# Shift and scale of the conditioning by output columns: two chunks of channels at a time, against all eight at once

## The chip, the cores and the metric

The kernel runs on one core of one Trainium2 chip. The metric is the device time of one execution in microseconds; the median of three runs is given. Views of the trace come from one profiled execution.

## The reference, cut to what matters

One layer of a streaming encoder, for a prompt of 2048 tokens with one conditioning vector and for 8 sample sequences of 16 tokens with one vector each. All is float32, with a width of 1024.

```python
def _layer(x, c, ...):
    mod = jax.nn.silu(c) @ w_ada + b_ada                 # w_ada: 1024 x 6144
    sh1, sc1, gt1, sh2, sc2, gt2 = [m[:, None, :] for m in jnp.split(mod, 6, axis=-1)]
    h = _rmsnorm(x, g_pre_mix) * (1 + sc1) + sh1
    proj = h @ w_in                                      # 17 units of 128 output channels
    ...                                                  # pooling, 31-tap convolution, short convolution
    mix = jnp.concatenate([ya, yb, yc], axis=-1) @ w_out
    x = x + gt1 * _rmsnorm(mix, g_post_mix)
    h = _rmsnorm(x, g_pre_ffn) * (1 + sc2) + sh2
    f = (jax.nn.silu(h @ w_gate) * (h @ w_up)) @ w_down
    return x + gt2 * _rmsnorm(f, g_post_ffn), ...
```

## The kernel before, in words

The 17 tiles of 128 tokens (1 of samples, 16 of the prompt) are worked in six blocks, the first of two tiles and the others of three. Every weight is streamed again for each block, as units of 128 x 1024, through a ring of six places (`raw`, `wlo` in the same memory, and `whi`). SP issues all loads, in an order written out by hand. A unit's place is loaded again once `w_used` counts its last reader. ScalarE makes the high part of a unit (`high(n)`, line 788), VectorE the rest (`low(n)`, line 1141), and TensorE (PE) takes three matmuls for each product of 128 rows: high by high, high by low, low by high (line 518). `ahead(...)` makes both parts four units ahead.

Each engine runs its own queue in program order and waits on semaphores. The modulation comes from `w_ada`: `ada_units` (line 539) multiplies four chunks of 128 input channels at a time, in four strips of the array, and leaves partial sums in four strips of PSUM; `ada_out` on ScalarE (line 939) copies them to `mod`; `ada_columns` (line 518) adds the four strips by a matmul with a matrix of ones and turns the result to channels by rows; `columns` on VectorE (lines 1152 to 1156) adds the bias and makes the scale. Parts 0 and 1 (shift and scale of the first norm) need the first sixteen units of `w_ada`, of 512 KB each. They go to `raw`, `h_pre` and `pr`. The others come later in fours, between projections.

For each chunk k of 128 channels of a block, `transposes(q, k)` on PE (line 573) turns the normalised x to channels by tokens in PSUM bank k % 2. In block 0 VectorE then scales and shifts the samples' tokens (`modulate_samples`, lines 1175 and 1177), ScalarE the prompt's (`modulate`, line 843) and splits off the high part (`h_split`, line 850), and VectorE makes the rest (`h_rest`, line 1183). `project(b, j)` is one unit of `w_in`. Its result is copied out of PSUM by `evacuate(b, j)` on ScalarE (lines 859 to 866), and unit j + 2 waits for that.

The convolutions and the pooling of a block are one generator on VectorE, `mixing(b)`, with 148 steps in block 0 (a step is one operation of the generator, the taps at line 1274 most of them). `advance(mixer, n)` takes n steps of it between other work. Its constants: `IN_FIRST` steps for each of the 15 units with an `ahead` in block 0, and again behind each of the four units in `FOUR_IN`; `IN_BETWEEN` steps before each `h_rest(1, k)`; `IN_EARLY` steps after each of four `low` while block 1's first units are projected; then `finish(mixer)` takes what is left. Pooling is the last part of it. On PE `statistics(0, i)` stand behind `project(1, 3)` and wait for `pooled_ready` and `z_ready`, which the generator signals; behind them come `project(1, 4)`, `gate_rows(0)`, `statistics(0, 3)`, `project(1, 5)`, `gate_rows(1)` and the first output projection, `mix_out(0, 0)`.

Of the kernel before, what the change touches and what calls it, by code (L numbers as in the profile page):

```python
# [11 lines left out]
P = 128  # L12
# [54 lines left out]

PRE = 2 * KD
PART_READ = {part: n for n, part in enumerate((0, 1, 3, 4, 2, 5))}
# [34 lines left out]
IN_FIRST, IN_BETWEEN, IN_EARLY, IN_OUT = 5, 3, 6, 2  # L104
# [13 lines left out]
E_END = E_FOLD + ROWS + 1  # L118
# [60 lines left out]
def build(nc, x_all, c_all, consts, consts_a, cols, gpost, b_ada, w_ada, w_mix, w_pool, w_gu, w_dn,  # L179
# [3 lines left out]
    with ctx:  # L183
# [8 lines left out]
        with ExitStack() as under:  # L192
            h_pre = sb("h_pre", [P, 2 * TB, D], scope=under, align=OPERAND)
# [59 lines left out]
        pre_landed = [sem(f"pre_landed{i}") for i in range(PRE)]  # L253
# [63 lines left out]
        def pre(i):  # L317

            if i < RING:
                return raw[:, i, :]  # L320
            i -= RING
            if i < 2 * TB:
                return h_pre[:, i, :]
            i -= 2 * TB
            return pr[:, :, :].rearrange("p s n -> p (s n)")[:, i * D:(i + 1) * D]

# [28 lines left out]

        def gu_bank(m, i):
            return (6 if m % 2 else 0) + i
# [4 lines left out]
        def _(sp):  # L362
# [34 lines left out]
            for i in range(STRIPS):  # L397
                sp.dma_start(pre(i), w_ada[i]).then_inc(pre_landed[i], 16)
# [5 lines left out]
            for i in range(STRIPS, PRE):  # L404
                sp.dma_start(pre(i), w_ada[i]).then_inc(pre_landed[i], 16)  # L405
# [37 lines left out]
            sp.wait_ge(cols_full, 2)  # L443
# [72 lines left out]
        def _(pe):  # L516
# [6 lines left out]
            def ada_units(q):  # L523

                g, k0 = STRIPS * q // KD, STRIPS * q % KD
                if k0 == 0 and g > 1:
                    pe.wait_ge(ada_read, PART_READ[g] - 1)
                if q >= PRE // STRIPS:
                    pe.wait_ge(four_landed[FOURS.index(q)], 16 * STRIPS)
                for h in range(2):  # L530
                    for i in range(STRIPS):
                        at, strip = STRIPS * q + i, C_PAD * i
                        if at < PRE:
                            src = pre(at)
                            if h == 0:
                                pe.wait_ge(pre_landed[at], 16)
                        else:
                            src = four_place(FOURS.index(q), i)
                        last = nc.tensor.matmul(ps[strip:strip + C_PAD, 2 + 2 * ADA_PAIR[g] + h, :], c_s[:, k0 + i, :],  # L539
                                                src[:, 512 * h:512 * h + 512], start=k0 == 0,  # L540
                                                stop=k0 + STRIPS == KD, tile_position=(0, strip), skip_group_check=True)
                        if h and at < PRE:
                            last.then_inc(pre_used, 1)
                if q >= PRE // STRIPS:
                    last.then_inc(four_used, 1)

            def ada_columns(bank):
                for i in range(2):
                    for k in range(KD):
                        o = (i * KD + k) * (ROWS + 1)  # L550
                        last = mm(ps[:, bank, o:o + ROWS + 1], mod[:, i, k * P:(k + 1) * P],
                                  con_a[0:MOD_K, E_FOLD:E_FOLD + ROWS + 1], True, True)
                last.then_inc(cols_full, 1)

            def gate_rows(i):

                e, row = E_SELP if i % 2 else E_SELS, PART_ROW[5 if i >= 2 else 2]
                pe.wait_ge(ada_read, PART_READ[5 if i >= 2 else 2] + 1)
                if i:
                    pe.wait_ge(gates_made, i)  # L560
                else:
                    pe.wait_ge(mod_ready, 4)
# [25 lines left out]
            def project(b, j):  # L588
                n, q, w = UNIT["in", b, j], norm("M", b), NT[b] * P
                if j >= 2:  # L590
                    pe.wait_ge(evac_done, evac_count(b, j - 2))
                elif b == 1:
# [4 lines left out]
                by_columns(n, ps[:, j % 2, 0:w], q, w, j == 0)  # L597
# [70 lines left out]
            def statistics(b, i):  # L668
# [3 lines left out]
                if i < NPOOL:  # L672
                    if b == 0 and i == 0:
                        pe.wait_ge(w_pool_landed, 16 * len(WINDOWS))
                        pe.wait_ge(ada_read, 6)
# [19 lines left out]
            for q in range(3):  # L695
                ada_units(q)
            pe.wait_ge(const_landed, 48)
            transposes(0, 0)
            transposes(0, 1)
            ada_units(3)  # L700
            pe.wait_ge(bias_landed[0], 16)
            pe.wait_ge(ada_read, 2)
            ada_columns(6)
            for k in range(2, KD):
                transposes(0, k)
            for j in range(NIN):
                project(0, j)
                if j in FOUR_IN:
                    ada_units(FOURS[FOUR_IN[j]])
# [3 lines left out]
            ada_units(FOURS[4])  # L713
# [3 lines left out]
            pe.wait_ge(ada_read, 4)  # L717
            ada_columns(7)
            for k in range(5, KD - 1):
                transposes(1, k)  # L720
            ada_units(FOURS[5])
# [3 lines left out]
            ada_units(FOURS[FOUR_EARLY[1]])  # L725
            project(1, 2)
            project(1, 3)
            ada_units(FOURS[FOUR_EARLY[3]])
# [53 lines left out]
        def _(act):  # L782
# [50 lines left out]
            def modulate(q, k):  # L833
                kind, b = NORMS[q]
                ph, w, c0 = int(kind == "F"), NT[b] * P, P if b == 0 else 0
                if k == 0:
                    act.wait_ge(mod_ready, 2 + 2 * ph)
# [14 lines left out]
            def evacuate(b, j):  # L852
# [3 lines left out]
                src = ps[:, j % 2, 0:w]  # L856
# [74 lines left out]
            nc.scalar.activation(c_s[:, :, 0:ROWS], c_sb[:, :, :], ACT.Silu).then_inc(c_ready, 1)  # L931
            def ada_out(g):
                if g < 2:
                    act.wait_ge(pre_used, KD * g + KD)
                else:
                    act.wait_ge(four_used, FOURS.index(2 * g + 1) + 1)
                if g > 2:
                    act.wait_ge(cols_full, 2 if g == 5 else 1)
# [7 lines left out]
            ada_out(0)  # L946
            ada_out(1)
            for n in range(LEAD):
                high(n)
            for k in range(KD):  # L950
                modulate(0, k)
                h_split(0, k)
                if k >= KD - 2:
                    high(LEAD + k - (KD - 2))
# [170 lines left out]
        def _(dve):  # L1125
# [22 lines left out]
            def columns(i, bank):  # L1148
                dve.wait_ge(cols_full, i + 1)
                src = ps[:, bank, 0:2 * KD * (ROWS + 1)].rearrange("p (n m) -> p n m", m=ROWS + 1)  # L1150
                dst = shsc[:, 2 * i:2 * i + 2, :, :].rearrange("p i k r -> p (i k) r")
                after(own.step(nc.vector.tensor_copy(dst, src[:, :, 0:ROWS])))
                tt(dst, dst, src[:, :, ROWS:ROWS + 1].to_broadcast([P, 2 * KD, ROWS]), ALU.add).then_inc(mod_ready, 1)
                g0 = (Q_G1, Q_G2)[i]
                dve.wait_ge(mod_ready, (1, 3)[i])
                stt(shsc[:, 2 * i + 1, :, :], shsc[:, 2 * i + 1, :, :], 1.0,
                    col[:, g0:g0 + KD].unsqueeze(2).to_broadcast([P, KD, ROWS]), ALU.add, ALU.mult)\
                    .then_inc(mod_ready, 1)
# [7 lines left out]
            def modulate_samples(q, k):  # L1166
                ph = int(NORMS[q][0] == "F")
                if k == 0:
                    dve.wait_ge(mod_ready, 2 + 2 * ph)
# [288 lines left out]
            for k in range(KD):  # L1458
# [16 lines left out]
            for k in range(KD):  # L1475
                advance(mixer, IN_BETWEEN)
                h_rest(1, k)
                if k == 5:
                    columns(1, 7)
# [178 lines left out]
```

## Time and profile before

| | us |
|---|---|
| median of three runs | 2311.78 (2310.27 to 2313.1) |
| the profiled execution's own time | 2310.73 |
| its span in the trace | 2308.9 |
| PE busy (matmul) | 2261.1, 98% of the span |
| VectorE busy | 1350.8, 59% |
| ScalarE busy | 1027.1, 44% |
| mean granted clock of TensorE | 0.99 |

The span runs from the first to the last record of the trace. A busy share is an average over the span; a stretch in which PE is idle has to be looked for in the time slices and the waits. The granted clock is the share of 2.4 GHz that PE got.

### The profile page before, as it was taken

How to read it: one execution, taken by the hardware profiler on the slowest of the kernel's cores; microseconds unless marked ns; L12 is line 12 of the kernel's file. 1: busy time of each engine (PE TensorE's matmuls, PEld its weight loads, DVE VectorE, ACT ScalarE, POOL GpSimd, SP SyncE). 2: the span in 40 equal slices, each digit the busy share in tenths (PEclk: the TensorE clock that was granted, in tenths of full speed). 3: DMA queues.
4: the chain of work that ended last, by engine and by line, in shares of the span. 5: the costliest groups of instructions: out<-in, count | busy, mean ns of one | idle time of the engine just before them, and what ended most of it. 6: DMA issues, size and time to landing. Idle time of an engine off the chain costs nothing.

```text
span 2308.9 us, 30258 instructions
## 1 busy us (share of the span) xinstructions
PE 2261.1 (98%) x12444; PEld 2084.0 (90%) x12444; DVE 1350.8 (59%) x1937; ACT 1027.1 (44%) x1432; POOL 41.6 (2%) x82
## 2 busy tenths in 40 slices
PE   7899999999999999999999999999999999999998
PEld 3779898988999998999998899989889997899987
DVE  3969885589453577744367764346784534443343
ACT  4554455545353534444353436344443424433332
POOL 0000000000000000000000000000000000000000
PEclk8999999999999999999999999999999999999999
DMA  8845454444533353453343354335335433444332
GB/s 334 335 151 173 166 201 153 158 171 164 183 125 122 127 183 120 155 174 127 128 176 127 127 183 146 128 119 182 128 123 178 127 125 117 173 153 155 128 128 91
DMA packets 101743, 361.64 MB, mean 157 GB/s; under 512 B 12259, under 2 KB 14435, under 8 KB 101604
## 3 DMA queue, kind: packets, MB, share of 16 engines
q1 hardware_dynamic: 101606, 359.71, 44.4%
q8 instruction: 99, 1.62, 0.3%
q14 instruction: 38, 0.31, 0.0%
HBM read 340.73 MB, written 18.93 MB: 156 GB/s over the span
## 4 chain that ended last, share of the span: by engine, by line
PE 90%; DVE 6%; DMA 2%; ACT 1%; SPq 1%; issue 0%; POOL 0%; POOLq 0%; DVEq 0%; ACTq 0%
PE ps L518 89%; DVE pr L1274 2%; DVE wlo L1141 2%; PE ps L573 1%; DMA raw<-in_w_mix 1%; DMA pr<-in_w_ada 1%; PE ps L539 0%; DVE h_lo L1183 0%; DVE g_lo L1190 0%; DMA raw<-in_w_gu 0%; SPq L405 0%; ACT whi L788 0%; DVE xr L1214 0%; ACT h_f L843 0%; DVE h_f L1175 0%
## 5 line engine op out<-in xcount | busy, mean ns | idle before, releaser
L1141 DVE TENSOR_TENSOR wlo<-raw,whi 128x1024 fp32r<-128x1024 f32 x546 | 665.1, 1223 | 524.8 <-ACT whi L788 523.6
L518 PE MATMUL ps<-h_hi,whi 128*128 128x384 f32 (+1 forms) x2928 | 960.0, 328 | 1.6 <-ACT h_f L843 1.6
L518 PE MATMUL ps<-h_lo,whi 128*128 128x384 f32 (+1 forms) x2928 | 954.8, 326 | 0.0
L518 PE MATMUL ps<-h_hi,wlo 128*128 128x384 f32 (+1 forms) x2928 | 954.8, 326 | 0.0
L788 ACT ACTIVATE whi<-raw 128x1024 fp32r<-128x1024 f32 x546 | 575.5, 1057 | 779.1 <-DMA raw<-in_w_gu 528.1
L518 PEld LDWEIGHTS ps<-h_hi,whi 128*128 128x128 f32 x2928 | 553.3, 189 | 9.1 <-issue 4.7
L518 PEld LDWEIGHTS ps<-h_lo,whi 128*128 128x128 f32 x2928 | 553.3, 189 | 2.2 <-issue 0.5
L518 PEld LDWEIGHTS ps<-h_hi,wlo 128*128 128x128 f32 x2928 | 553.2, 189 | 0.0
L518 PE MATMUL ps<-whi,g_hi 128*128 128x512 f32 x748 | 235.9, 396 | 7.0 <-DVE g_lo L1190 5.5
L518 PE MATMUL ps<-whi,g_lo 128*128 128x512 f32 x748 | 231.6, 391 | 0.0
L518 PE MATMUL ps<-wlo,g_hi 128*128 128x512 f32 x748 | 231.2, 390 | 0.0
L1274 DVE SCALAR_TENSOR_TENSOR pr<-u,col,pr 128x384 f32<-128x384 f32 x360 | 208.8, 614 | 0.9
L1565 DVE TENSOR_TENSOR g_f<-ps,s_buf 128x384 f32<-128x384 f32 (+1 forms) x132 | 70.5, 534 | 222.4 <-PE ps L518 222.2
L518 PEld LDWEIGHTS ps<-whi,g_hi 128*128 128x128 f32 x748 | 137.3, 189 | 36.7 <-DVE g_lo L1190 9.8
L518 PEld LDWEIGHTS ps<-wlo,g_hi 128*128 128x128 f32 x748 | 140.7, 188 | 30.0
L518 PEld LDWEIGHTS ps<-whi,g_lo 128*128 128x128 f32 x748 | 140.7, 188 | 29.8
L843 ACT ACTIVATE h_f<-ps,shsc 128x384 f32<-128x384 f32 (+1 forms) x96 | 61.0, 635 | 223.3 <-PE ps L573 196.7
L1183 DVE TENSOR_TENSOR h_lo<-h_f,h_hi 128x384 fp32r<-128x384 f32 (+1 forms) x96 | 51.4, 535 | 154.2 <-ACT h_hi L850 154.2
L518 PE MATMUL ps<-whi,y_pr 128*128 128x512 f32 x476 | 137.2, 395 | 0.0
L859 ACT ACTIVATE pr<-ps 128x384 f32<-128x384 f32 (+1 forms) x84 | 39.4, 469 | 146.1 <-PE ps L518 146.1
L518 PEld LDWEIGHTS ps<-whi,y_pr 128*128 128x128 f32 x476 | 87.8, 188 | 17.6 <-issue 0.5
L1190 DVE TENSOR_TENSOR g_lo<-g_f,g_hi 128x384 fp32r<-128x384 f32 (+1 forms) x132 | 70.1, 531 | 11.3 <-ACT g_hi L927 11.3
(127 smaller groups left out, 1192.7 us busy)
## 6 DMA issues: line engine op xcount, KB each, us to landing
raw<-in_w_gu SPq DMA_DIRECT2D x264, 512.0 KB, 3.2
raw<-in_w_mix SPq DMA_DIRECT2D x150, 512.0 KB, 3.3
raw<-in_w_dn SPq DMA_DIRECT2D x132, 512.0 KB, 3.2
xt<-in_x_all SPq DMA_DIRECT2D x17, 512.0 KB, 5.9
xr<-in_x_all SPq DMA_DIRECT2D x17, 512.0 KB, 6.0
xr<-x_all SPq DMA_DIRECT2D x17, 512.0 KB, 5.6
x_all<-xr SPq DMA_DIRECT2D x5, 1536.0 KB, 7.5
xr<-in_w_ada SPq DMA_DIRECT2D x12, 512.0 KB, 6.8
```

The source lines that it names most:

```text
L518: return nc.tensor.matmul(out, lhsT, rhs, start=start, stop=stop, skip_group_check=True)
L573: last = nc.tensor.transpose(ps[:, k % 2, t * P:(t + 1) * P], xt[:, t, k * P:(k + 1) * P], ident)
L788: nc.scalar.activation(whi[:, s, :], raw[:, s, :], ACT.Copy).then_inc(w_hi, 1)
L843: nc.scalar.activation(h_f[:, k % 2, c0:w], ps[:, k % 2, c0:w], ACT.Identity, scale=shsc[:, 2 * ph + 1, k, 0:1], bias=shsc[:, 2 * ph, k, 0 ...
L859: i = nc.scalar.activation(dst, src, ACT.Sigmoid if kind == "g" else ACT.Copy)
L1141: tt(wlo[:, s, :], raw[:, s, :], whi[:, s, :].bitcast(F32), ALU.subtract).then_inc(w_lo, 1)
L1183: tt(h_lo[:, k, 0:w], h_f[:, k % 2, 0:w], h_hi[:, k, 0:w].bitcast(F32), ALU.subtract)\
L1190: tt(g_lo[:, s, 0:w], g_f[:, k, 0:w], g_hi[:, s, 0:w].bitcast(F32), ALU.subtract).then_inc(g_lo_ready, 1)
L1274: i = stt(z, conv_in(j, k), wk, src, ALU.mult, ALU.add)
L1565: tt(g_f[:, m, 0:w], ps[:, gu_bank(m, 1), 0:w], s_buf[:, m % 2, 0:w], ALU.mult).then_inc(g_ready, 1)
```

## The change

The first sixteen units of `w_ada` are laid out in DRAM by output columns: four groups of four units, a group holding all input channels for two chunks of shift and two of scale. `ada_group(g)` multiplies a group whole (8 matmuls of 512 columns) into one PSUM bank of its own; `group_out(g)` copies that bank; `group_columns(g)` takes 4 small matmuls for the two chunks; `columns` takes the same two chunks. Each group's chunks are transposed, modulated and split while the next group lands. The bias is added by the matmul itself, so that `columns` has two operations and not three. The landing place is one tensor, `pre`, over `h_hi`, `h_lo`, `raw` and a part of `pr`. Units 0 and 1 of block 0 go to PSUM banks 2 and 3. Further, `high` and `low` of units 0 to 5 stand at the last group and behind it, the states are loaded behind unit 5 instead of unit 3, `load_x(1)` stands behind unit 8 instead of unit 5, and `IN_FIRST` goes from 5 to 4 and `IN_BETWEEN` from 3 to 1.

```diff
-PART_READ = {part: n for n, part in enumerate((0, 1, 3, 4, 2, 5))}
+GROUPS = PRE // STRIPS
+PART_READ = {part: GROUPS + 1 + n for n, part in enumerate((3, 4, 2, 5))}
...
-IN_FIRST, IN_BETWEEN, IN_EARLY, IN_OUT = 5, 3, 6, 2
+IN_FIRST, IN_BETWEEN, IN_EARLY, IN_OUT = 4, 1, 6, 2
...
-            h_pre = sb("h_pre", [P, 2 * TB, D], scope=under, align=OPERAND)
+            pre = sb("pre", [P, PRE, D], scope=under, align=OPERAND)
...
+        def in_bank(b, j):
+
+            return j % 2 + (2 if b == 0 and j < 2 else 0)
...
-                    sp.wait_ge(pre_used, n + 1)
+                    sp.wait_ge(pre_used, (2 * TB + n) // STRIPS + 1)
...
-                if j == 3:
+                if j == RING - 1:
                     sp.dma_start(u_s[:, :, 0:SEQS, :], st_conv).then_inc(state_landed, 16)
...
                 if j == RING - 1:
                     load_four(0)
-                    sp.wait_ge(t_full, KD)
-                    load_x(1)
                 if j == 7:
                     load_four(1)
                 if j == 8:
-                    sp.wait_ge(cols_full, 1)
+                    sp.wait_ge(t_full, KD)
+                    load_x(1)
+                    sp.wait_ge(cols_full, GROUPS)
...
+            def ada_group(g):
+
+                pe.wait_ge(pre_landed[g], 16 * STRIPS)
+                for k in range(KD):
+                    strip = C_PAD * (k % STRIPS)
+                    out = ps[strip:strip + C_PAD, 2 + g, :].rearrange("p (a n) -> p a n", a=STRIPS)
+                    last = nc.tensor.matmul(out, c_s[:, k, :], pre[:, STRIPS * g:STRIPS * g + STRIPS, k * P:(k + 1) * P],
+                                            start=k < STRIPS, stop=k >= STRIPS, tile_position=(0, strip),
+                                            skip_group_check=True)
+                last.then_inc(pre_used, 1)
...
+            def group_columns(g):
+                pe.wait_ge(ada_read, g + 1)
+                if g >= 2:
+                    pe.wait_ge(mod_ready, 2 * (g - 1))
+                ada_columns(6 + g % 2, (2 * g, 2 * g + 1))
...
-            for q in range(3):
-                ada_units(q)
+            ada_group(0)
             pe.wait_ge(const_landed, 48)
-            transposes(0, 0)
-            transposes(0, 1)
-            ada_units(3)
             pe.wait_ge(bias_landed[0], 16)
-            pe.wait_ge(ada_read, 2)
-            ada_columns(6)
-            for k in range(2, KD):
-                transposes(0, k)
+            for g in range(GROUPS):
+                group_columns(g)
+                if g + 1 < GROUPS:
+                    ada_group(g + 1)
+                transposes(0, 2 * g)
+                transposes(0, 2 * g + 1)
...
+            def group_out(g):
+                act.wait_ge(pre_used, g + 1)
+                src = ps[0:BIAS, 2 + g, :].rearrange("p (i n) -> p i n", i=2)
+                nc.scalar.activation(mod[0:BIAS, 0:2, 2 * P * g:2 * P * (g + 1)], src, ACT.Copy).then_inc(ada_read, 1)
...
+            group_out(0)
             for t in range(NT[0]):
                 x_square(0, t)
             for t in range(NT[0]):
                 x_normalise(0, t)
-            ada_out(0)
-            ada_out(1)
-            for n in range(LEAD):
+            for g in range(GROUPS):
+                if g:
+                    group_out(g)
+                if g == GROUPS - 1:
+                    high(0)
+                for k in (2 * g, 2 * g + 1):
+                    modulate(0, k)
+                    h_split(0, k)
+            for n in range(1, RING):
                 high(n)
...
-            for n in range(2):
-                low(n)
-            columns(0, 6)
-            modulate_samples(0, 0)
-            for k in range(KD):
-                if k + 1 < KD:
-                    modulate_samples(0, k + 1)
-                h_rest(0, k)
-                if k in (3, 5):
-                    low(2 + k // 5)
-            for n in range(LEAD, RING):
+            for g in range(GROUPS):
+                columns(0, 6 + g % 2, (2 * g, 2 * g + 1))
+                modulate_samples(0, 2 * g)
+                modulate_samples(0, 2 * g + 1)
+                if g == GROUPS - 1:
+                    low(0)
+                h_rest(0, 2 * g)
+                h_rest(0, 2 * g + 1)
+            for n in range(1, RING):
                 low(n)
...
-    wa = np.asarray(w_ada)[0].reshape(KD, P, 6, D).transpose(2, 0, 1, 3).reshape(6 * KD, P, D)
+    wa = np.asarray(w_ada)[0].reshape(KD, P, 6, D).transpose(2, 0, 1, 3)
+    wa_groups = wa[:2].reshape(2, KD, P, GROUPS, 2, P).transpose(3, 0, 4, 2, 1, 5).reshape(PRE, P, D)
+    wa = np.concatenate([wa_groups, wa[2:].reshape(4 * KD, P, D)])
```

## Rows read from the trace of the kernel before

**Rows 1.** The page, busy time of each engine over the span.
```profile
PE 2261.1 (98%) x12444; PEld 2084.0 (90%) x12444; DVE 1350.8 (59%) x1937; ACT 1027.1 (44%) x1432; POOL 41.6 (2%) x82
```
**Rows 2.** Stretches: length, then PE, PEld, DVE, ACT, POOL busy, clock, DMA share, GB/s.
```profile
65.88:113.11 47.23, 42.82 (x353) 34.97 (x344) 47.16 (x101) 27.02 (x42) 2.14 (x2) 0.98 0.87 321
118.55:148.17 29.62, 28.86 (x170) 22.73 (x169) 20.16 (x56) 10.14 (x15) 0.00 (x0) 0.89 0.30 107
...
167.02:2308.90 2141.88, 2120.62 (x11574) 1979.52 (x11572) 1248.41 (x1702) 948.38 (x1309) 37.78 (x72) 1.00 0.42 147
```
**Rows 3.** Waits of PE, 50 to 400 us: total, times, longest.
```profile
PE ps L573 <- ACT h_f L843: 8.7, 7, 5.2
```
**Rows 4.** Chain of waits in order of time, 0 to 140 us: start, length, what.
```profile
12.93 14.97 DMA pr<-in_w_ada
...
29.89 1.03 ACT mod L939
...
31.05 5.05 PE ps L518 x32
...
45.87 10.82 PE ps L518 x72
...
56.71 8.06 DMA raw<-in_w_mix
```
**Rows 5.** Timeline of PE, 0 to 75 us: start, length, operation, idle before.
```profile
17.95 0.62 PE L539 MATMUL ps<-h_pre,c_s 128*32 128x512 f32 x1 [0.16 <-DMA h_pre<-in_w_ada]
...
24.77 0.66 PE L573 MATMUL ps<-con,xt 128*128 128x128 f32 x4
```
**Rows 6.** Timeline of ACT (ScalarE), 0 to 75 us.
```profile
15.61 2.19 ACT L817 ACTIVATE xt<-xt,rstd_x 128x1024 f32<-128x1024 f32 x2 [1.16 <-POOL rstd_x L1081]
...
37.81 0.46 ACT L843 ACTIVATE h_f<-ps,shsc 128x128 f32<-128x128 f32 x1 [3.12 <-DVE h_f L1177]
...
39.10 0.42 ACT L850 ACTIVATE h_hi<-h_f 128x256 fp32r<-128x256 f32 x1
```
**Rows 7.** Timeline of DVE (VectorE), 0 to 185 us.
```profile
37.08 0.29 DVE L1175 TENSOR_TENSOR h_f<-ps,shsc 128x128 f32<-128x128 f32 x1
...
65.88 1.23 DVE L1141 TENSOR_TENSOR wlo<-raw,whi 128x1024 fp32r<-128x1024 f32 x1 [3.93 <-ACT whi L788]
...
143.78 1.23 DVE L1141 TENSOR_TENSOR wlo<-raw,whi 128x1024 fp32r<-128x1024 f32 x1 [3.14 <-ACT whi L788]
...
147.11 0.60 DVE L1352 SCALAR_TENSOR_TENSOR pr<-wsum,xa 64x128 f32<-64x128 f32 x2
```
**Rows 8.** Stretches of 1 us, as rows 2; the clock is the third number from the end.
```profile
33.00:34.00 1.00, 1.00 (x7) 1.00 (x7) 1.00 (x2) 1.00 (x2) 0.00 (x0) 0.59 1.11 388
...
111.00:112.00 1.00, 0.00 (x0) 0.00 (x0) 1.00 (x5) 0.00 (x0) 0.00 (x0) 0.84 1.03 410
```
**Rows 9.** Timeline of PE, 100 to 205 us.
```profile
105.70 0.87 PE L573 MATMUL ps<-con,xt 128*128 128x128 f32 x6 [0.54 <-ACT xa L864]
...
149.48 1.10 PE L518 MATMUL ps<-pr,w_pl 128*128 128x256 f32 x4 [1.19 <-issue]
...
160.14 1.56 PE L518 MATMUL ps<-pr,con_a 128*128 128x256 f32 x6 [2.38 <-ACT pr L885]
...
167.02 1.03 PE L518 MATMUL ps<-whi,y_pr 128*128 128x512 f32 x2
```
**Rows 10.** Chain of waits in order of time, 100 to 170 us.
```profile
114.48 0.90 PE ps L573 x3
115.39 6.63 PE ps L518 x32
...
127.46 8.60 PE ps L518 x48
...
146.43 1.90 PE ps L539 x16
...
150.14 7.57 DMA raw<-in_w_mix
```

More of the change, by code:

```diff
@@ L252, in build @@
         w_pool_landed = sem("w_pool_landed")
-        pre_landed = [sem(f"pre_landed{i}") for i in range(PRE)]
+        pre_landed = [sem(f"pre_landed{i}") for i in range(GROUPS)]
         pre_used = sem("pre_used")
@@ L397, in _ @@
             for i in range(STRIPS):
-                sp.dma_start(pre(i), w_ada[i]).then_inc(pre_landed[i], 16)
+                sp.dma_start(pre[:, i, :], w_ada[i]).then_inc(pre_landed[0], 16)
             load_x(0)
@@ L404, in _ @@
             for i in range(STRIPS, PRE):
-                sp.dma_start(pre(i), w_ada[i]).then_inc(pre_landed[i], 16)
+                sp.dma_start(pre[:, i, :], w_ada[i]).then_inc(pre_landed[i // STRIPS], 16)
             def load_four(f):
@@ L525, in ada_units @@
+            def ada_units(f):
+                q = FOURS[f]
                 g, k0 = STRIPS * q // KD, STRIPS * q % KD
[L526 to L529, printed above, removed]
+                if k0 == 0:
+                    pe.wait_ge(ada_read, max(GROUPS, PART_READ[g] - 2))
+                pe.wait_ge(four_landed[f], 16 * STRIPS)
                 for h in range(2):
@@ L531, in ada_units @@
                     for i in range(STRIPS):
[L532 to L538, printed above, removed]
+                        strip = C_PAD * i
                         last = nc.tensor.matmul(ps[strip:strip + C_PAD, 2 + 2 * ADA_PAIR[g] + h, :], c_s[:, k0 + i, :],
-                                                src[:, 512 * h:512 * h + 512], start=k0 == 0,
+                                                four_place(f, i)[:, 512 * h:512 * h + 512], start=k0 == 0,
@@ L541, in ada_units, with ada_columns @@
                                                 stop=k0 + STRIPS == KD, tile_position=(0, strip), skip_group_check=True)
[L542 to L547, printed above, removed]
+                last.then_inc(four_used, 1)
+            def ada_columns(bank, ks):
                 for i in range(2):
-                    for k in range(KD):
-                        o = (i * KD + k) * (ROWS + 1)
-                        last = mm(ps[:, bank, o:o + ROWS + 1], mod[:, i, k * P:(k + 1) * P],
-                                  con_a[0:MOD_K, E_FOLD:E_FOLD + ROWS + 1], True, True)
+                    for n, k in enumerate(ks):
+                        o = (i * len(ks) + n) * ROWS
+                        last = mm(ps[:, bank, o:o + ROWS], mod[:, i, k * P:(k + 1) * P],
+                                  con_a[0:MOD_K, E_FOLD:E_FOLD + ROWS], True, True)
@@ L591, in project @@
                     pe.wait_ge(evac_done, evac_count(b, j - 2))
+                elif b == 0:
+                    pe.wait_ge(ada_read, j + 1)
                 elif b == 1:
@@ L712, in _ @@
             transposes(1, 1)
-            ada_units(FOURS[4])
+            ada_units(4)
             for k in range(2, 5):
@@ L716, in _ @@
             pe.wait_ge(bias_landed[1], 16)
-            pe.wait_ge(ada_read, 4)
-            ada_columns(7)
+            pe.wait_ge(ada_read, PART_READ[4])
+            ada_columns(7, range(KD))
             for k in range(5, KD - 1):
                 transposes(1, k)
-            ada_units(FOURS[5])
+            ada_units(5)
             transposes(1, KD - 1)
@@ L724, in _ @@
             project(1, 1)
-            ada_units(FOURS[FOUR_EARLY[1]])
+            ada_units(FOUR_EARLY[1])
             project(1, 2)
             project(1, 3)
-            ada_units(FOURS[FOUR_EARLY[3]])
+            ada_units(FOUR_EARLY[3])
             for i in range(3):
@@ L835, in modulate @@
                 ph, w, c0 = int(kind == "F"), NT[b] * P, P if b == 0 else 0
-                if k == 0:
-                    act.wait_ge(mod_ready, 2 + 2 * ph)
+                if q == 0:
+                    act.wait_ge(mod_ready, 2 * (k // 2) + 2)
+                elif k == 0:
+                    act.wait_ge(mod_ready, 2 * GROUPS + 2 * ph)
                 act.wait_ge(t_full, KD * q + k + 1)
@@ L945, in _ @@
                 x_normalise(0, t)
-            ada_out(0)
-            ada_out(1)
-            for n in range(LEAD):
-                high(n)
[L950 to L954, printed above, removed]
+            for g in range(GROUPS):
[7 more added lines that the diff above has]
+            for n in range(1, RING):
+                high(n)
             for j in range(NIN):
@@ L1146, in ahead, with columns @@
                     low(n)
[L1148 to L1158, printed above, removed]
+            def columns(i, bank, ks):
+                n = len(ks)
+                dve.wait_ge(cols_full, ks[0] // 2 + 1 if i == 0 else GROUPS + 1)
+                src = ps[:, bank, 0:2 * n * ROWS].rearrange("p (i k r) -> p i k r", i=2, r=ROWS)
+                at, g0 = slice(ks[0], ks[0] + n), (Q_G1, Q_G2)[i] + ks[0]
+                nc.vector.tensor_copy(shsc[:, 2 * i, at, :], src[:, 0, :, :]).then_inc(mod_ready, 1)
+                stt(shsc[:, 2 * i + 1, at, :], src[:, 1, :, :], 1.0,
+                    col[:, g0:g0 + n].unsqueeze(2).to_broadcast([P, n, ROWS]), ALU.add, ALU.mult).then_inc(mod_ready, 1)
             def gate(i, bank):
@@ L1167, in modulate_samples @@
                 ph = int(NORMS[q][0] == "F")
-                if k == 0:
-                    dve.wait_ge(mod_ready, 2 + 2 * ph)
+                if k % 2 == 0 if q == 0 else k == 0:
+                    dve.wait_ge(mod_ready, 2 * GROUPS + 2 if ph else k + 2)
                 dve.wait_ge(t_full, KD * q + k + 1)
@@ L1478, in _ @@
                 if k == 5:
-                    columns(1, 7)
+                    columns(1, 7, range(KD))
             for j in range(EARLY - 2):
```

35 lines of the change are left out of this document (11 added, 24 removed).

## The prediction, made before the change was run

> **What bounds the kernel now.** Read the page's engine rows first: PE is busy 98% of the span [rows 1]. The table of stretches then splits the execution where the first output projection begins. From 167.02 us to the end PE is busy 2120.62 of 2141.88 us at a granted clock of 1.00 [rows 2], and the edit touches nothing there. So the change is worth what it does to one moment, the start of `mix_out(0, 0)`, which I call M: 167.02 us now. Everything after M should move with it. PE's waits after 50 us show the largest of them in the transposes of block 1 [rows 3].
>
> Next read the chain of waits for the prologue [rows 4]. The last chunk of `w_ada` is awaited until 27.90. Then come the copy of the modulation, 5.05 us of small matmuls in `ada_columns`, and two exchanges of VectorE and ScalarE per chunk of channels. The first unit of `w_in` starts at 45.87. The reader is to see that 45.87 − 27.90 = 18 us are a serial tail behind the load.
>
> **The start, part by part.** The diff makes four groups of two chunks. Their loads are the same sixteen in the same order, so the eighth still lands at 17.95 and the last at 27.90 [rows 4, 5]. What follows per group is a chain, because `group_out(g+1)` stands behind both chunks of group g on ScalarE, and `group_columns(g+1)` stands ahead of `ada_group(g+2)` on PE. At full clock one period is:
> - 8 matmuls of 512 columns (16 instructions): 1.90, as a four-chunk unit takes at 146.43;
> - first transposes, two tiles: 0.66 / 2 = 0.35 [rows 5];
> - sample part on VectorE, two operations of 0.3: 0.65 with the hand-over;
> - two modulate and split pairs: 37.81 to the end of 39.10 + 0.36, 1.65 [rows 6];
> - `group_out`, 105x512: not in the trace; between 0.46 for 128x128 with scale and bias [rows 6] and 1.03 for 105x1024 [rows 4]. I take 0.60, between them and a little over half of the latter;
> - 8 of the 32 column instructions: between 5.05 / 32 and less, since that burst ran partly at the lower clock. I take 0.105 each at full clock, 0.85, with 0.1 to hand over.
>
> Sum 6.1, against 5.0 for a group's four loads (a load each 1.25 us, [rows 4, 5]). So the groups aren't hidden under the loads: the chain paces them. From 17.95: `ada_group(1)` ends 19.85, `ada_group(2)` 25.95, `ada_group(3)` 32.05. The same links bring `group_columns(3)` to 36.3. Then VectorE's two small operations of `columns` 0.5 (the transposes, 0.35, beside them), both sample parts 1.2 and `low(0)` 1.2, which is put ahead of `h_rest(0, 6)` [rows 7], give a first projection at 39.2. `group_out(0)` now stands ahead of the squares of x on ScalarE. That is hidden: the normalised x is there at 17.80 [rows 6] and `ada_group(1)` ends 2 later. Behind the start `high(1)` and `low(1)` need 2.3 us, which unit 0 covers (24 matmuls of 0.12, 2.9); `evacuate(0, 0)` stands behind `high(5)`, some 5.9 after it, when unit 2 is due at 5.8 to 8: 0 to 0.5. Banks 2 and 3 for units 0 and 1 take away a wait for the last read of banks 0 and 1, which `low(0)` outlasts: nothing. The removed third operation of `columns` and the dropped tenth column are inside these figures, under 0.4 us.
>
> All TensorE terms double at the lower level. Period then 3.8 + 0.7 + 0.65 + 1.65 + 0.6 + 1.8 = 9.2, and the start is 48.6. Which is it? The granted clock fell from 2.4 to 1.2 GHz at 33.2 (0.59 over that microsecond), after PE had done nothing since 29.86 but the columns, and at 111.7 after nothing since 109.24 [rows 8]. In the change every period has such a stretch between two dense bursts, with only columns and transposes in it. The bursts themselves are as dense as now. So I expect both levels in turn, and take a start near the middle, 43.5, 2.4 earlier than now. Ends for the range: 39.2 and 48.6.
>
> **What the queue does next.** In SP's order `load_x(1)` moves from before unit 6 to behind unit 8, in front of unit 9. It sat in a stretch where the queue was idle; now 3 x 512 KB stand in a full one. Unit 8 landed at 64.77 (56.71 + 8.06, [rows 4]); it is issued by a use count, so it lands at 62.4. Four transfers of 512 KB at the 1.25 us each that back-to-back loads take bring unit 9 to 67.4. `high(9)` 1.06, and `low(9)` starts at 68.6. On ScalarE `high(9)` stands ahead of `evacuate(0, 5)`, for which unit 7 waits: that ends 69.0, PE would be there at 67.5, so PE stalls 1.5. The last unit of block 0 ends at 105.2 − 2.4 + 1.5 = 104.3 (the transposes now start 105.70, [rows 9]). If that stall is covered, 1.5 comes off. The later permission for units 0 to 5 costs nothing: unit 0 lands right behind the last `w_ada` load, near 29.2, and `high(0)` isn't reached before 34. If SP were late, each microsecond would be one of start. The states, loaded two units later, are first needed by the mixer, 15 us on.
>
> VectorE must keep up. From `low(8)` at 65.88 to the first `h_rest` of block 1, 47.23 us, it was busy all the time, with 13 `low` of 1.14 and 85 mixer steps, so 0.38 a step [rows 2, 7]. Now 12 `low` and 64 steps follow `low(9)`: 38.1. Done 106.7. One step and `h_rest(1, 0)` later, 107.6, ScalarE modulates chunk 2 (0.7), and transposes of chunk 4 start at 108.4, where PE is ready too. They started at 114.48 [rows 10]: the 5.25 us stall goes, and 6.1 us are gained here.
>
> From there to the first projection of block 1 took 127.46 − 114.48 = 13.0, most of it at the lower clock: the columns of the second half took 6.63 [rows 10]. At full clock it would be 0.45 + 32 x 0.105 + 0.87 (six transposes, [rows 9]) + 1.90 + 0.35 + 0.75 (modulate, hand-over) = 7.7. The stall before is shorter now, so part of it runs fast: 11. The projection starts at 119.4, 8 earlier.
>
> **Where it is given back.** `IN_FIRST` 5 to 4 and `IN_BETWEEN` 3 to 1 take 19 + 16 = 35 mixer steps out of the part before that point. The mixer has 148 steps. Before, 143 were issued by the end of the early loop and 5 were left; now 108 are issued and 40 are left. They come after `low(24)`, which waits for PE: it started at 143.78, 16.3 after the projection [rows 7, 10]. The last 40 steps are what VectorE did from 118.55 to 148.17: 20.16 busy [rows 2] less 4 `low` (4.6), 4 `h_rest` (1.9) and `columns` (0.8) = 12.9. So both pooled halves are ready 16.3 + 1.1 + 6 x 0.38 + 12.9 − 0.5 = 32.1 after the projection, at 151.5; now that is 147.7 (147.11 + 0.60, [rows 7]). PE reaches `statistics(0, 0)` at 119.4 + 20.9 = 140.3 (146.43 + 1.90 − 127.46 = 20.9, four projections and two units of four, [rows 10]) and cannot pass: `pooled_ready` is the last product of the mixer. It waits some 11 us, with one short matmul in between.
>
> From the statistics to M now: 149.48 to 167.02, 17.5 [rows 9]. Of it 0.4 is the first statistic, which is done earlier, and 2.4 a wait that ends at a weight load, issued at 150.14 behind `gpost` and the residual tiles, landing 7.57 later [rows 10]. That load is issued at 140 now and is hidden. After an 11 us stall the clock is low: the two other statistics, 8 instructions of 0.2 at full rate, and what follows until it rises, 1.7 more (0 if it doesn't fall, 3 if it stays down into the projection). 17.5 − 0.4 − 2.4 + 1.7 = 16.4, M = 167.9. Add 0.9 to the profiled execution: 2310.73 (the span of 2308.9 and 1.8 around it, which stay) + 0.9 = 2311.6. The median of the runs stands 1.05 above that execution, so 2312.7.
>
> **The rivals.** About 0.2%, 4.6 us, is what a measurement of this kernel can tell from no change.
> First, the lower clock throughout the start. For it: each gap between bursts is like the stretches behind which the clock fell before [rows 8]. Against it: four-chunk bursts may lift it again. The start is at 48.6, 5.1 later than I take, and M is 173.0: 2317.8, slower. It decides from a start of 47.2, 3.7 above mine.
> The page "TensorE: Matmul & The Clock Gate" of the Trainium skill, section "HAM oscillation — how this bites in real kernels", describes just this: bursts with waits for loads between them begin cold each time. By that rule the time would be the 2317.8 of this rival; the trace of before agrees only so far as its two falls do.
> Second, full clock throughout, start at 39.2, and the 2.2 us that the first units lose now won as well (their 72 matmuls took 10.82 [rows 4]; 256 columns at two thirds of 8.60 / 48 each are 8.6): M 6.5 earlier, 161.4, 2306.2, faster. Against it: the same rows.
> Third, the mixer's rest hides: PE finds the pooled tiles ready, and M is 140.3 + 18.7 = 159.0, 2303.8. The order on VectorE speaks against it: the 46 steps behind `low(24)` take 15 us, and they would have to be done within 4.
>
> **How the numbers follow.** Forecast, no change that can be told: 0.58, its own range 2308 to 2317. Low clock, slower: 0.20. Full clock: 0.16. Hidden rest: 0.06. Faster is 0.16 + 0.06 = 0.22, same 0.58, slower 0.20. The range that leaves out 2 in 10 runs from 2306 to 2318.5; the bounds of the transposes-to-projection term (7.7 to 13.0) lie in it.
>
> **What would show it.** Right: a first projection at 41 to 46, dense bursts of 1.9 to 3.8 in the start, the stall at 109 to 114 reduced, and a new PE wait of 8 to 14 us on the pooling operations near 140 to 151. Unit 9 would land near 67. Wrong: no such wait, or M more than 4.6 from 167. I would be wrong if the steps left over are shorter than their rows, or if the projection of block 1 starts before 115.

## The result

The change made the kernel slower. The median of 8 runs is 2320.39 us (2317.41 to 2324.54) against 2312.93 for the kernel before (8 runs, 2310.27 to 2316.5); the ratio is 1.0035, 95% interval 1.0025 to 1.0044. Run again beside other kernels it gave 1.0034, 1.0022 to 1.0047. The forecast was 2312.7 with a range up to 2318.5, and no change that can be told as the likeliest case.

The page of the changed kernel, busy time of each engine, to be held against [rows 1]:

```profile
PE 2259.0 (97%) x12444; PEld 2085.6 (90%) x12444; DVE 1351.2 (58%) x1941; ACT 1026.9 (44%) x1434; POOL 41.6 (2%) x82
```

The work is the same, the span is 11 us longer (2319.9 against 2308.9). The table of stretches, as [rows 2], from just behind the first output projection to the end:

```profile
175.00:2319.90 2144.90, 2122.16 (x11573) 1980.90 (x11571) 1247.86 (x1701) 948.45 (x1309) 38.78 (x72) 1.00 0.42 147
```

PE is as full there as before. M, the start of `mix_out(0, 0)`, went from 167.02 to 174.62, by 7.6 us, and the medians differ by 7.5. The other 3.4 us of the two profiled spans lie behind M. In the eleven profiled executions below, the part behind M took 2142.9 to 2146.2 us, whatever was changed ahead of it, and the profiled execution of before, with 2141.9, was a low one. So I count M and the medians, not the two spans.

Now the start. Timeline of PE in the changed kernel, to be held against [rows 5]:

```profile
9.73 3.64 PE L526 MATMUL ps<-pre,c_s 128*32 128x512 f32 x16 [9.73 <-DMA pre<-in_w_ada]
14.17 1.85 PE L515 MATMUL ps<-con_a,mod 106*128 106x9 f32 x8 [0.80 <-ACT mod L942]
18.06 3.64 PE L526 MATMUL ps<-pre,c_s 128*32 128x512 f32 x16 [2.04 <-DMA pre<-in_w_ada]
21.64 0.79 PE L578 MATMUL ps<-con,xt 128*128 128x128 f32 x4
25.29 1.83 PE L515 MATMUL ps<-con_a,mod 106*128 106x9 f32 x8 [2.86 <-ACT mod L942]
27.06 3.64 PE L526 MATMUL ps<-pre,c_s 128*32 128x512 f32 x16
...
34.38 1.06 PE L515 MATMUL ps<-con_a,mod 106*128 106x9 f32 x8 [2.64 <-ACT mod L942]
35.37 3.46 PE L526 MATMUL ps<-pre,c_s 128*32 128x512 f32 x16
...
42.38 1.85 PE L515 MATMUL ps<-con_a,mod 106*128 106x9 f32 x8 [2.85 <-ACT mod L942]
44.08 1.09 PE L578 MATMUL ps<-con,xt 128*128 128x128 f32 x4
47.22 0.55 PE L515 MATMUL ps<-h_hi,whi 128*128 128x256 f32 x1 [2.05 <-issue]
```

The group bursts (L526) take 3.64 and 3.46 us, the length at the lower clock (1.92 at the full one, as e4 shows below), and none starts on a landing after the second. The third starts at 27.06 and the fourth at 35.37; the same loads landed at about 22.9 and 27.9 before, and in e5, where these bursts wait for nothing else, they start at 23.41 and 28.41. Each waits behind the columns, and these for `group_out` on ScalarE (mod L942). The first projection starts at 47.22, 1.35 later than before. The granted clock, in stretches of 2 us (third number from the end), shows why the later bursts are slow:

```profile
18.00:20.00 2.00, 1.94 (x12) 0.60 (x16) 0.00 (x0) 1.59 (x2) 0.00 (x0) 1.00 1.03 422
...
24.00:26.00 2.00, 0.71 (x4) 0.71 (x4) 0.84 (x2) 1.21 (x3) 0.00 (x0) 0.84 1.02 418
26.00:28.00 2.00, 2.00 (x14) 1.32 (x17) 0.26 (x2) 0.00 (x0) 0.00 (x0) 0.50 1.03 424
28.00:30.00 2.00, 2.00 (x16) 0.31 (x8) 0.00 (x0) 0.00 (x0) 0.00 (x0) 0.50 0.68 279
30.00:32.00 2.00, 1.75 (x8) 0.72 (x4) 0.56 (x3) 0.00 (x0) 0.00 (x0) 0.50 0.10 33
32.00:34.00 2.00, 0.00 (x0) 0.00 (x0) 1.07 (x5) 1.79 (x5) 0.00 (x0) 0.95 0.95 356
...
36.00:38.00 2.00, 2.00 (x16) 0.44 (x8) 0.00 (x0) 0.00 (x0) 0.00 (x0) 0.50 0.97 385
38.00:40.00 2.00, 1.53 (x8) 0.52 (x4) 0.56 (x3) 0.00 (x0) 0.00 (x0) 0.74 1.08 380
40.00:42.00 2.00, 0.00 (x0) 0.00 (x0) 1.07 (x5) 1.80 (x5) 0.00 (x0) 1.00 1.06 429
```

The first row must be read with care. Ahead of the first change that this trace shows, at 25 us, the clock stands at 1.00, but the second burst took 3.64 us there, as long as under 0.50; for the first two bursts the level is known only from their lengths. In the later rows the level follows the burst and so comes too late: PE gets 0.50 while the third burst runs and 0.95 in the idle stretch behind it, and the same again for most of the fourth. The phase is not the same in each execution: in e11, the same kernel again, the clock stays at 0.50 from 30 to 36 us, the idle stretch included. The lengths are the same: of the twenty bursts in the profiled executions of the changed kernel, e1, e3, e9 and e11, which share this start, each took 3.33 to 3.64 us. At 30 to 32 the load queue is nearly empty too (33 GB/s): units 2 to 5 of `w_in` wait for `pre_used` of the late third group.

Block 0's units, timeline of ScalarE (the splits that waited for a load), against unit 8 at 64.77 before [rows 4]:

```profile
66.64 1.06 ACT L793 ACTIVATE whi<-raw 128x1024 fp32r<-128x1024 f32 x1 [4.85 <-DMA raw<-in_w_mix]
...
71.73 1.06 ACT L793 ACTIVATE whi<-raw 128x1024 fp32r<-128x1024 f32 x1 [3.76 <-DMA raw<-in_w_mix]
...
106.33 1.06 ACT L793 ACTIVATE whi<-raw 128x1024 fp32r<-128x1024 f32 x1 [2.89 <-DMA raw<-in_w_mix]
```

The second is unit 9, 5.1 us behind unit 8 with the three tiles of x between them. Before, it had no wait. Then the statistics, in the waits of PE from 50 to 400 us, as [rows 3]:

```profile
PE ps L515 <- DVE pr L1360: 11.4, 3, 7.2
PE ps L578 <- ACT h_f L850: 5.8, 7, 2.0
```

The wait for the transposes shrank from 8.7 to 5.8 in total, and a new one of 11.4 stands for the last operations of pooling. Timeline of PE there, against [rows 9]:

```profile
125.74 0.44 PE L515 MATMUL ps<-h_hi,whi 128*128 128x384 f32 x1 [0.76 <-ACT h_f L850]
...
153.72 1.19 PE L515 MATMUL ps<-pr,w_pl 128*128 128x256 f32 x2 [7.15 <-DVE pr L1360]
158.32 1.22 PE L515 MATMUL ps<-pr,w_pl 128*128 128x256 f32 x2 [3.41 <-DVE pr L1360]
159.34 2.73 PE L515 MATMUL ps<-pr,con_a 128*128 128x256 f32 x6
...
174.62 1.03 PE L515 MATMUL ps<-whi,y_pr 128*128 128x512 f32 x2
```

### The profile page after: what moved, and what is told of

Its sections match the earlier page's. It is cut to its first block, busy times and chain, and to the rows that moved or that the text cites. A ratio compares the mean times of both kernels' runs of the same rounds, so it can differ in the third digit from the quotient of the medians.

```text
span 2319.9 us, 30274 instructions
## 1 busy us (share of the span) xinstructions
PE 2259.0 (97%) x12444; PEld 2085.6 (90%) x12444; DVE 1351.2 (58%) x1941; ACT 1026.9 (44%) x1434; POOL 41.6 (2%) x82
## 4 chain that ended last, share of the span: by engine, by line
PE 90%; DVE 6%; DMA 2%; ACT 1%; issue 1%; SPq 0%; POOL 0%; POOLq 0%; ACTq 0%; DVEq 0%
PE ps L515 88%; DVE wlo L1152 2%; DVE pr L1282 1%; PE ps L578 1%; DMA raw<-in_w_mix 1%; DMA raw<-in_w_gu 1%; DMA pre<-in_w_ada 0%; PE ps L541 0%; DVE g_lo L1198 0%; ACT whi L793 0%; DVE h_lo L1191 0%; ACT h_f L850 0%; DVE xr L1222 0%; PE ps L526 0%; DVE pr L1304 0%
```

## The experiments

The milestones are of each kernel's profiled execution; start is that of the first projection, "block 1" that of `project(1, 0)`.

| kernel | median | before in the same job | ratio (95%) | start | block 1 | M |
|---|---|---|---|---|---|---|
| before | 2312.93 | | | 45.87 | 127.46 | 167.02 |
| changed | 2320.39 | 2312.93 | 1.0035 (1.0025 to 1.0044) | 47.22 | 125.74 | 174.62 |
| e1 | 2318.61 | 2313.76 | 1.0022 (1.0013 to 1.0031) | 47.26 | 131.47 | 170.96 |
| e2 | 2316.15 | 2313.76 | 1.0014 (1.0005 to 1.0023) | 45.91 | 119.64 | 168.76 |
| e3 | 2318.22 | 2313.76 | 1.0022 (1.0014 to 1.0030) | 47.38 | 126.05 | 174.62 |
| e4 | 2314.30 | 2313.76 | 1.0006 (0.9997 to 1.0015) | 42.29 | 118.04 | 166.65 |
| e5 | 2310.33 | 2313.78 | 0.9981 (0.9972 to 0.9990) | 36.14 | 117.03 | 167.00 |
| e6 | 2304.60 | 2313.78 | 0.9965 (0.9952 to 0.9977) | 35.34 | 120.51 | 161.64 |
| e7 | 2311.66 | 2313.78 | 0.9996 (0.9987 to 1.0005) | 41.87 | 121.28 | 163.84 |
| e9 | 2316.22 | 2313.78 | 1.0010 (1.0001 to 1.0019) | 47.83 | 130.56 | 171.72 |
| e10 | 2314.51 | 2312.11 | 1.0010 (1.0001 to 1.0019) | 46.35 | 130.59 | 171.63 |
| e11 | 2320.54 | 2312.11 | 1.0034 (1.0022 to 1.0047) | 48.43 | 127.85 | 177.84 |
| e12 | 2306.14 | 2312.11 | 0.9969 (0.9958 to 0.9981) | 33.82 | 118.75 | 158.34 |

How far one profiled execution can be trusted shows in two pairs. The changed kernel and e11 are the same kernel, and their M is 174.62 and 177.84; e6 and e12 are the same kernel, with 161.64 and 158.34. So a difference of M of some 3 us between two kernels is not told by one pair of traces, and where M and the ratio disagree the ratio counts. The profiled execution was the fastest run of its kernel in e2, e4 and e12, and the slowest in e3, e5, e6 and e11. The changed kernel was timed in another set of runs than e1 to e4, so its ratio is compared with theirs, not its median.

**e1: the old step counts in the changed kernel.**

```diff
-IN_FIRST, IN_BETWEEN, IN_EARLY, IN_OUT = 4, 1, 6, 2
+IN_FIRST, IN_BETWEEN, IN_EARLY, IN_OUT = 5, 3, 6, 2
```

> The changed kernel with the old step counts (IN_FIRST 5, IN_BETWEEN 3), the groups and the moved load of x kept. Theory A, steps left over: in the changed kernel the mixer's 40 steps behind the early loop hold PE at the statistics for some 11 us (pooled at 158.3 us, first output projection at 174.6). With 5 left over, the first h_rest of block 1 comes about 6 us later, block 1's projection starts near 130, but pooling is done when PE gets there, and the first output projection starts near 169.5. Time about 5 us below the changed kernel, near 2315. Rival B, it is the late start and the moved load alone that cost: the first output projection stays at 174 to 175, same time as the changed kernel or a few us worse, since block 1 starts later.

Block 1 starts 5.7 us later, and M is 3.7 earlier. The long wait for pooling is gone: 0.9 us is left of the 11.4. The ratio falls from 1.0035 to 1.0022. M alone would not decide against rival B, being near the spread above, but with the vanished wait and the lower ratio it is out. The gain, some 3 us by the ratios, is smaller than the 5 expected.

**e2: the new step counts alone, in the kernel before** (the same line the other way round).

> The kernel before with only the step counts changed (IN_FIRST 4, IN_BETWEEN 1). Theory A: block 1's projection starts earlier (near 120 and not 127.5), but PE then waits about 11 us at the statistics for pooling, which is ready 32 us after that start, near 152; first output projection near 168.5 against 167.0. Time 1 to 2 us above before. Rival B: the counts are harmless or help; time at or below before, down to 7 us below, where pooling does not hold PE.

Waits of PE, 50 to 400 us, in e2:

```profile
PE ps L518 <- DVE pr L1352: 11.4, 3, 7.1
PE ps L573 <- ACT h_f L843: 5.3, 7, 1.5
```

Block 1 at 119.64 and M at 168.76 are what was expected, and the wait for pooling is that of the changed kernel. The ratio, 1.0014, is clear of 1; the median is 2.4 us above before, a little more than the 1 to 2 expected. The counts alone win 7.8 us at block 1 and lose 9.6 behind it.

**e3: `load_x(1)` back behind unit 5, in the changed kernel.**

```diff
                 if j == RING - 1:
                     load_four(0)
+                    sp.wait_ge(t_full, KD)
+                    load_x(1)
...
                 if j == 8:
-                    sp.wait_ge(t_full, KD)
-                    load_x(1)
                     sp.wait_ge(cols_full, GROUPS)
```

> The changed kernel with load_x(1) back behind unit 5, where the load queue is idle. Theory A: unit 8 and unit 9 of block 0 land some 1 and 5 us earlier (unit 9 at about 66.5 and not 71.7), VectorE's steps of block 0 run 2 to 4 us earlier, and with them everything behind: first output projection 2 to 4 us earlier, time 2 to 4 us below the changed kernel. Rival: the landing was not on the path (the units were needed later): no change of time.

The time fell as expected, by some 3 us (1.0035 to 1.0022), though the two intervals overlap. The milestones don't show it: M is 174.62 as before the edit. The profiled execution, 2322.61, was the slowest of this kernel's 12 runs. In it unit 9 no longer waits for its load: its split starts at 67.91, where it was 71.73. The transposes of chunk 4 start 1.3 us earlier than in the changed kernel (113.34 against 114.64), and 1.6 are lost again up to block 1, at the lower clock. This run alone leaves the load open; e10 was made for it.

**e4: PE kept busy in the gaps.** The added matmuls go into a bank that nothing reads.

```diff
+            def keep_busy(n):
+                for _ in range(n):
+                    mm(ps[:, 2, 0:E_CNT], con_a[:, 0:P], con_a[:, 0:E_CNT], True, True)
...
                 group_columns(g)
+                if g == 0:
+                    keep_busy(3)
...
                 transposes(0, 2 * g + 1)
+                if g + 1 < GROUPS:
+                    keep_busy(6)
```

> The changed kernel with unneeded float32 matmuls of 384 columns on PE in the gaps between the groups of the start (3 behind the first columns, 6 behind each of the three later pairs of transposes), into a PSUM bank that nothing reads; results are unchanged. Theory A, the lower clock paces the groups: granted clock near 1.00 from about 20 us on, ada groups of 1.9 and not 3.6 us, first projection near 41 and not 47.2, first unit not at half rate, time 5 to 7 us below the changed kernel. Rival: the exchanges of VectorE and ScalarE pace the groups, or the added matmuls take what the clock gives: first projection within 1.5 us of 47, time the same or higher.

Timeline of PE in e4:

```profile
18.15 1.92 PE L526 MATMUL ps<-pre,c_s 128*32 128x512 f32 x16 [0.86 <-DMA pre<-in_w_ada]
20.01 0.66 PE L578 MATMUL ps<-con,xt 128*128 128x128 f32 x4
20.50 4.04 PE L515 MATMUL ps<-con_a 128*128 128x384 f32 x12
24.37 0.96 PE L515 MATMUL ps<-con_a,mod 106*128 106x9 f32 x8
25.26 1.92 PE L526 MATMUL ps<-pre,c_s 128*32 128x512 f32 x16
```

The same bursts take 1.92 and not 3.64, the columns 0.96 and not 1.83, and the granted clock is 1.00 in all stretches from 14 to 46 us. The time is 7 us below the changed kernel. The clock paced the groups, as theory A has it. The filler was mis-sized: 4.04 where the gap is 2.9, so a period is 7.1 us. Without the 1.1 too much it would be some 6.0 (an estimate), near the 6.1 forecast for full clock and above the 5.0 of a group's loads.

**e5: the queues of the start reordered.** Nothing is added to hold the clock; the order that makes the chain is changed.

```diff
-            for g in range(GROUPS):
-                group_columns(g)
-                if g + 1 < GROUPS:
-                    ada_group(g + 1)
+            group_columns(0)
+            ada_group(1)
+            for g in range(GROUPS):
+                if g:
+                    group_columns(g)
                 transposes(0, 2 * g)
                 transposes(0, 2 * g + 1)
+                if g + 2 < GROUPS:
+                    ada_group(g + 2)
...
             for g in range(GROUPS):
-                if g:
-                    group_out(g)
-                if g == GROUPS - 1:
+                if g + 1 < GROUPS:
+                    group_out(g + 1)
+                if g == GROUPS - 2:
                     high(0)
...
-                if g == GROUPS - 1:
+                if g == GROUPS - 2:
                     low(0)
```

> The changed kernel with the queues of the start reordered and nothing else: ada_group(g + 2) stands on PE right behind the transposes of group g, group_out(g + 1) on ScalarE ahead of the modulation of group g, high(0) and low(0) one group earlier. Theory A, the order makes a chain of about 9 us per group at the lower clock: out of it, the last group is multiplied right behind its landing (about 28 to 32.5 us) and the first projection starts near 39, 8 us earlier; pooling, still with 40 steps left over, and the first output projection come 7 to 8 earlier (near 167), time within 2 us of the kernel before. Rival: the groups are paced by the loads or by VectorE; first projection above 44, no gain.

Timeline of PE in e5:

```profile
23.41 1.92 PE L526 MATMUL ps<-pre,c_s 128*32 128x512 f32 x16 [0.55 <-DMA pre<-in_w_ada]
25.27 1.06 PE L515 MATMUL ps<-con_a,mod 106*128 106x9 f32 x8
26.18 0.63 PE L578 MATMUL ps<-con,xt 128*128 128x128 f32 x4
28.41 2.87 PE L526 MATMUL ps<-pre,c_s 128*32 128x512 f32 x16 [1.60 <-DMA pre<-in_w_ada]
```

Now the third and fourth burst wait for their loads and for nothing else. The start is at 36.14, 11 us earlier and 3 better than expected. Not all of it is the order: the clock came out higher too, with the third burst at 1.92 and the fourth at 2.87. An estimate for the lower clock throughout: the third burst ends at 27.05, the columns (1.85) and transposes (1.1) behind it at 30.0, so the fourth starts 1.6 later and takes 0.8 longer, and the first projection comes near 38.5. That leaves nearly 9 of the 11 us to the order. M is at 167.00, the same as before, and yet the median is 3.4 us below before, where at most 2 was expected; the profiled execution was the slowest of 11. The wait for pooling is still there (11.8 us).

**e6 and e12: e5 with the old step counts and the old place of `load_x(1)`.**

> The reordered start together with the old step counts (5, 3) and the old place of load_x(1). Theory A: first projection near 39, no long wait at the statistics; first output projection near 161, time 5 to 7 us below the kernel before and 12 below the changed one. Rival: VectorE is then the bound of block 0 and eats the start: first output projection at 165 or later.

> The reordered start with the old step counts and the old place of load_x(1) once more, the best version so far: 8 to 9 us below the kernel before, if its start near 35.5 us and its first output projection near 160 come again.

The best version: 0.35% and, again, 0.31% below the kernel before. By the medians that is 9.2 and 6.0 us, where 5 to 7 and then 8 to 9 had been expected. Start 35.34 and 33.82, M 161.64 and 158.34. Here VectorE's backlog at the transposes of block 1 is the largest wait of PE (6.0 us at once in e6, 4.3 in e12); the first statistic waits 1.2 and the last 2.3 to 2.4, as in the kernel before.

**e7: e4 with the same two edits.**

> The kernel with matmuls in the gaps, with the old step counts and the old place of load_x(1). Theory A: first projection near 42.3 at full clock, first output projection near 162, time about 4 below the kernel before. Rival: as for the reordered start.

M 163.84 and 2.1 us below before, which the interval (0.9987 to 1.0005) does not tell from nothing. I had expected 4. PE waits 3.78 us at the last statistic, 1.5 more than in e6, and runs on at the lower clock, as it does in e6. What made that wait longer wasn't followed.

**e9: the changed kernel with both edits**, so that the start by groups alone is left.

> The changed kernel with old step counts and old place of load_x(1): what is left is the start by groups alone. Theory A: first projection at 47.3, 1.4 later than before, and some 2 later after the half rate of its first unit; first output projection near 168.5 to 169, time 1.5 to 2.5 us above the kernel before. Rival: the start by groups costs more than its shift, through loads of units 0 to 8 that come later: first output projection above 170.

The time is as expected, 2.4 above before. M is not: 171.7, where 168.5 to 169 was expected, and above the 170 named for the rival. But start and transposes are both 2.0 behind those of before, so nothing is lost between them to late loads; the other 2.7 are lost where PE restarts at the lower clock behind waits, which it does for longer here than in the trace of before. One trace doesn't tell whether that belongs to the kernel or to the execution.

**e10: `load_x(1)` moved alone, in the kernel before.**

```diff
                 if j == RING - 1:
                     load_four(0)
-                    sp.wait_ge(t_full, KD)
-                    load_x(1)
...
                 if j == 8:
+                    sp.wait_ge(t_full, KD)
+                    load_x(1)
                     sp.wait_ge(cols_full, 1)
```

> The kernel before with one edit: load_x(1) behind unit 8 of block 0 and not behind unit 5. Theory A: three loads of 512 KB now stand in a full queue; unit 9 lands some 4 to 5 us later than now, VectorE, which is behind with the steps of block 0, waits for it, and the first output projection starts 1.5 to 3 us later; time 1.5 to 3 us above before. Rival: the units land early enough, no change.

Timeline of ScalarE in e10, units 8 and 9:

```profile
65.22 1.06 ACT L788 ACTIVATE whi<-raw 128x1024 fp32r<-128x1024 f32 x1 [4.96 <-DMA raw<-in_w_mix]
70.24 1.06 ACT L788 ACTIVATE whi<-raw 128x1024 fp32r<-128x1024 f32 x1 [3.69 <-DMA raw<-in_w_mix]
```

Unit 9 lands 5.0 behind unit 8, as in the changed kernel, and the time is 2.4 above before. M is 171.63, 4.6 later where 1.5 to 3 was expected; the ratio, 1.0010, bears out the 2.4 and not the 4.6.

**e11: the changed kernel again.**

> The changed kernel once more, beside the others of this job: 7 to 8 us above before if the first measurement holds. The sum of its parts taken alone, steps 2.4 (the kernel before with new counts), start by groups 2.4 (old counts and old load place) and x load (1.5 to 3), gives 6.3 to 7.8.

8.4 us above before, ratio 1.0034. The three parts taken alone give 0.14 + 0.10 + 0.10 = 0.34%. Each alone is just above what can be told from nothing, and the error of the sum is about 0.16%; the sum agrees with the whole measured twice, but it doesn't prove that the parts simply add.

## Why the prediction was wrong

It held the right parts and took one of them 4 us too early. Milestones, forecast against the changed kernel:

| | forecast | measured |
|---|---|---|
| first projection | 43.5 (39.2 to 48.6) | 47.22 |
| split of unit 9 | 67.4 | 71.73 |
| transposes of chunk 4, block 1 | 108.4 | 114.64 |
| from there to block 1 | 11 | 11.1 |
| block 1 to both pooled halves | 32.1 | 32.6 |
| from there to M | 16.4 | 16.3 |
| M | 167.9 | 174.62 |

**The start is the step that failed.** The term was a first projection at 43.5, midway between the two clock levels; it measured 47.22. I had both ends and the chain of each, and the end at the lower clock, 48.6, was nearly right. I took a start near the middle because the bursts are as dense as before and might lift the clock. They did lift it, but behind themselves: the stretches show 0.50 under the third burst and most of the fourth, and 0.95 to 1.00 in the gaps. A mean of the two levels was wrong: nearly all the work ran low, in all five executions with this start. That is 3.7 us. The first rival described this, with 47.2 as the start that decides for it and 2317.8 as its time, and I gave it 0.20. The rule of the Trainium skill that stands beside it ("TensorE: Matmul & The Clock Gate", section "HAM oscillation — how this bites in real kernels": bursts with waits between them start cold each time) fits two of the three later bursts, the second by its length; the fourth, at 35.37, began at full clock and was at 0.50 from 36 us on. e4 shows the cause: with the gaps filled the same bursts are half as long.

**The queue** was right in kind. Unit 9 came 5.1 behind unit 8 (5.0 forecast), e10 prices the move at 2.4 us, and the late start carried both. A second effect was not in the sum, which had VectorE busy all the way from the second part of unit 9 to block 1: near the end of block 0 a later split waits for its load until 106.33 (102.50 before), and VectorE stands idle for 1.96 us. Before, the split waited too, but VectorE still had steps to do. Every kernel with the new step counts has this idle time (1.35 us in e2, 2.47 in e3, 1.39 in e4, 2.16 in e5, 2.40 in e11), also where the load of x is in its old place (e2, e3), and none with the old counts has it. So it comes from the steps taken away and not from the moved load. With the 3.7 of the start and 0.6 at unit 9 it makes the 6.2 us at the transposes.

Timeline of VectorE in the changed kernel:

```profile
107.42 1.23 DVE L1152 TENSOR_TENSOR wlo<-raw,whi 128x1024 fp32r<-128x1024 f32 x1 [1.96 <-ACT whi L793]
```

**The steps left over** were right to half a microsecond: 32.6 from block 1 to pooling, 11 us of wait, 16.3 to M. I had sized their net effect as giving back what the earlier block 1 wins. e2 measures it alone: a loss of 0.14%, M 1.7 later.

**Full clock and hidden rest**, the two faster cases, are both out: the clock was low, and pooling held PE in every kernel with the new counts (e2, e3, e4, e5, e11). The range missed the median by 1.9 us. The forecast for M was 6.7 us short and that for the median 7.7, so nearly all of the error lies ahead of M; the rest is that the kernel before came out 1.1 higher over 8 runs (2312.93) than over 3. The start alone would have given 2316.4, inside the range. It took the idle VectorE and the smaller misses with it to go past 2318.5.

## What to carry to other kernels

A pipeline over engines is made by the order in each queue, not by the size of the pieces. Here the order (group g + 1 copied out behind all of group g) made the pieces a chain of 8 to 9 us against loads of 5; putting the next group's matmuls and copy ahead, and unit 0's split with them, won 11 us at the start, some 2 of them by the clock that rose with it. When bursts are cut up with gaps between them as here, cost them at the lower clock; don't take a mean. And when one wait is shortened by putting work off, look for the instruction that needs the last of that work: the 35 steps put off won 7.8 us at one wait and lost 9.6 at the next.

## What the runs showed of the hardware

The granted clock could be high exactly while PE had nothing to do: 0.95 to 1.00 at 32 to 34 and 40 to 42 us in the changed kernel, between bursts that ran at 0.50. Matmuls of 10 columns neither held nor raised the level: in the kernel before it fell at 33.2, 2 us into the 32 of them that start at 31.05, and it stayed at 0.50 through the 32 that start at 115.18 and take 6.84. A stretch ahead of the trace's first change of clock can read 1.00 while the matmuls take the time of the lower level (3.64 us for a burst that takes 1.92 at full clock). A copy of 105x512 from PSUM took 0.58 to 0.60 us on ScalarE (0.60 was taken), VectorE's operations on 128x18 took 0.17 and 0.18.
